# Two transformer blocks on one core: order of the first modulation, of one norm and of the merge's first gate

## The chip, the cores and the metric

The kernel runs on one core of a Trainium2 chip. The metric is the device time of one execution in microseconds, the median of several runs.

## The reference, cut to what matters

Two blocks follow each other on x of 512 tokens by 1024 channels, in float32. Cut to what the change touches:

```python
# first block
mod = silu(c) @ w_ada + b_ada                 # 1024 -> 6144
sh1, sc1, gt1, sh2, sc2, gt2 = split(mod, 6)
h = rmsnorm(x, g_mix) * (1 + sc1) + sh1
proj = h @ w_in                               # q, k, v, pool, gates of a convolution
...
x = x + gt1 * (concat(y_a, y_b, y_c) @ w_out)
h = rmsnorm(x, g_ffn) * (1 + sc2) + sh2
x = x + gt2 * ((silu(h @ w_gate) * (h @ w_up)) @ w_down)
# second block, after a final norm and a feed-forward: ya, yb are its two attentions
...
merged = sigmoid(ga) * (ya @ w_branch_a) + sigmoid(gb) * (yb @ w_branch_b)
h = h + merged @ w_out                        # then the third feed-forward and the last norm
```

`ga` and `gb` are columns of the second block's input projection.

## The kernel before

Activations lie channels by tokens: x is 8 blocks of 128 channels by 512 tokens. Every weight matrix comes in slabs (numbered 0 to 265, mostly 512 KB). Each product is made of three, high by high, high by low and low by high: `split_high(s)` on ScalarE (L1169) rounds a slab to its high half `w_hi`, `split_low(s)` on VectorE (L1567) makes `w_lo` and counts `w_ready`. `w_raw`, `w_hi` and `w_lo` have two buffers each, slab s in s % 2. SP loads slab s when slab s - 2 is split; `split_high(s)` waits until TensorE has used slab s - 2. TensorE's products are lines L564 to L566, whatever the slab. The input has halves too, `h_hi` (ScalarE) and `h_lo` (VectorE), counted by `h_ready`.

Each engine has one program in order, and they meet only at semaphores. PSUM banks are given out ahead of time by `plan`, with what completes and what frees each turn of a bank.

**First modulation.** `sh1` and `sc1` are made on TensorE from `ada_w`, in two halves h of 512 channels: `first_rows(h, ...)` is small products over eight pieces of `ada_w` (L613), `first_columns(h)` turns the row to columns (L624), VectorE (`copy_rows`, `first_mods`) makes the scale, and then for each block k VectorE makes `hm` (L1608), ScalarE `h_hi` (L1188) and VectorE `h_lo` (L1616). The second half's `first_rows(1)` stands inside slab 1 of the value projection (slabs 0 to 3, two blocks k each, four token tiles i each). The other parts of the modulation are summed on VectorE by `mod_step(r)` over rows of `w_ada` that SP brings; `mod_columns` on TensorE (L651) needs eight steps. Slabs 4 and 5 are the first of q and k.

**Norm of the first feed-forward.** The eight chunks `out1` (slabs 28 to 35) are added to x on VectorE (`add_gated`, L1780), squared on ScalarE (`sq`, L1321, two buffers), and summed on the pool engine (`acc`, L2131). TensorE sums over the channels with `mean_d` (L836), ScalarE takes the root (L1357), VectorE the reciprocal, TensorE spreads it over the channels (`spread`, L825), and VectorE and ScalarE make the blocks of h. In between TensorE does `warm(n)`, n products of the identity with itself (L591). Slabs 36 and 37 are the first gate and up slabs.

**Second attention's end and merge.** 32 units t of attention run with half a slab of the input projection each (`part`), scores (L982), transposes (L1000) one unit later, and every fourth unit the values are weighed (`weigh_values`, L957). The last unit's transposes are in round 32, the last weighing in round 33. Then follow per n = 0 to 7 the gate `gb` (slab 182 + 2n) and the two branches (slab 183 + 2n) in `gates`. SP, ScalarE and VectorE go through the slabs in order.

Of the kernel before, what the change touches and what calls it, by code (L numbers as in the profile page):

```python
# [134 lines left out]
def program(nc, ins, out):  # L135
    ctx = ExitStack()
    with ctx:
# [408 lines left out]
        def _(pe):  # L546
# [108 lines left out]
            for s in range(S_V, S_V + 4):  # L655
                await_slab(s)
                for i in range(TT):
                    if s == S_V + 1 and i == 2:
                        first_rows(1, range(KD))
                    if s == S_V + 1 and i == 3:  # L660
                        first_columns(1)
                    b = take(("v1", i)) if s == S_V else i
                    for j in range(2):
                        k = 2 * (s - S_V) + j
                        pe.wait_ge(h_ready, k + 1)
                        ts = slice(P * i, P * i + P)
                        ws = slice(T * j, T * j + T)
                        last = three(psum[:, b, :], h_hi[:, k, ts], h_lo[:, k, ts], w_hi[:, s % 2, ws],
                                     w_lo[:, s % 2, ws], k == 0, k == KD - 1)
                last.then_inc(w_used, 1)  # L670
# [159 lines left out]
            b = take(("sum", "ffn0"))  # L830
            for part_, ready in ((acc[:, 0, :], (summed, SUM0 + KD - 1)), (sq[:, 1, 0, :], (squared, KD))):
                if ready[0] is squared:
                    warm(10)
                pe.wait_ge(*ready)
                for i in range(TT):
                    last = pe.matmul(psum[:, b, i:i + 1], part_[:, P * i:P * i + P], mean_d,  # L836
                                     start=ready[0] is summed and i == 0, stop=ready[0] is squared, skip_group_check=True)
            last.then_inc(filled[b], 1)
            warm(6)
            spread(("scale", "ffn0"), 4, 1)  # L840
            warm(20)

# [99 lines left out]
            def weigh_values(g):  # L942
# [17 lines left out]
                last.then_inc(filled[b], 1)  # L960

            for t in range(UN2 + 2):
                if t < UN2:
# [38 lines left out]


            wait_emptied(pe, ("o2", UN2 // 4 - 1))
            ab = [(ya_hi[:, k, :], ya_lo[:, k, :]) for k in range(4)], [(yb_hi[:, k, :], yb_lo[:, k, :]) for k in range(4)]

            def gates(n, i=None):
                await_slab(S_MERGE + 2 * n, i, 2)
                b = take(("gb",), n, i)
                chunk(psum[:, b, :], S_MERGE, range(KD), hs).then_inc(w_used, 1)  # L1010
                await_slab(S_MERGE + 2 * n + 1, i, 2)
                b = take(("a",), n, i)
                chunk(psum[:, b, :], S_MERGE + 1, range(0, 4), ab[0]).then_inc(filled[b], 1)
                b = take(("b",), n, i)
                chunk(psum[:, b, :], S_MERGE + 1, range(4, 8), ab[1]).then_inc(w_used, 1)
# [141 lines left out]
        def _(act):  # L1157
# [27 lines left out]
            for h in range(PARTS):  # L1185
                for k in range(KP * h, KP * h + KP):
                    act.wait_ge(x_normed, k + 2)
                    act.activation(h_hi[:, k, :], hm[:, k % 2, :], ACT.Identity, bias=modc[:, SH1 + k:SH1 + k + 1])\  # L1188
                       .then_inc(h_high, 1)
                    if k == KP + 1:  # L1190
                        split_high(3)
                if h == 0:
                    split_high(1)
                    split_high(2)
# [318 lines left out]
        def _(dve):  # L1513
# [80 lines left out]
            for h in range(PARTS):  # L1594
# [6 lines left out]
                for k in range(KP * h, KP * h + KP + 1):  # L1601
                    if k == KP + 2:
                        split_low(3)
                    if k < KP * h + KP:
# [14 lines left out]
                if h == 0:  # L1619
                    split_low(1)  # L1620
                    b = wait_filled(dve, "late_vectors")
                    dve.tensor_copy(vcol[:, FIRST_ROWS:N_ROWS], psum[:, b, FIRST_ROWS:N_ROWS]).then_inc(emptied[b], 1)
            dve.wait_ge(lam_landed, 80)
            done(dve.tensor_tensor(lamrow[:, 128:192], lamrow[:, 0:64], lamrow[:, 64:128], ALU.mult))
# [12 lines left out]
            mod_step(1)  # L1637
            for s in range(4, 7):
                split_low(s)
                for r in range(2 * s - 6, 2 * s - 4):  # L1640
                    mod_step(r)
            mod_group(GT1 // KD, KD)

# [148 lines left out]
            for n in range(KD):  # L1792
                wait_emptied(dve, ("side", n))
                add_gated(("out1",), "out1", n, None, GT1)
                if n < KD - 1:
                    split_low(S_OUT1 + n + 2)

            def token_scale(name):
# [263 lines left out]
        def _(pool):  # L2062
# [46 lines left out]
            def sums(phase, clear, kinds=1):  # L2109
# [4 lines left out]
                else:  # L2114

                    pool.memset(acc[:, 0:kinds, :], 0.0).then_inc(summed, 1)
                    pool.wait_ge(summed, SUM0 + SQUARES[phase])
# [10 lines left out]
            pool.wait_ge(summed, SUM0)  # L2128
            for n in range(KD - 1):
                pool.wait_ge(squared, n + 1)  # L2130
# [85 lines left out]
```

## Time and profile before

| | us |
|---|---|
| median of 3 runs | 1731.37 |
| lowest, highest | 1730.52, 1734.26 |
| the profiled execution | 1731.43 |
| its span in the trace | 1729.6 |
| TensorE busy | 1692.3 |
| VectorE busy | 818.6 |
| ScalarE busy | 613.9 |
| pool engine busy | 144.9 |

The rows below come from that one profiled execution, in us from the start of its span. In the timeline a row has the start, the busy time of the instruction or of the merged group, engine, line, operation, output and inputs, the count, and in brackets the idle time ahead of it with what ended it. PE is TensorE, DVE VectorE, ACT ScalarE, POOL the pool engine, SPq the queue that issues transfers. PEclk is the granted clock of TensorE as a part of 2.4 GHz.

### The profile page before, as it was taken

The page shows a single profiled execution, that of the slowest core. Times are in us where ns is not written, and L with a number is a line of the kernel's source. Part 1 is how long each engine was busy: PE and PEld are TensorE (multiplying, and loading weights), DVE is VectorE, ACT ScalarE, POOL GpSimd, SP SyncE. Part 2 cuts the span into 40 slices and gives each one's busy share as a digit, 9 for nine tenths or more (in the row PEclk, how much of TensorE's full clock was granted, in tenths as well). Part 3 has the DMA queues.
Part 4 walks back from the last instruction along what each step waited for, and adds up shares of the span by engine and source line. Part 5 has one row for each costly group of instructions (what it writes and reads, how often), then busy time and mean ns, then how long its engine had stood idle before and what let it go on. Part 6 is the DMA issues. An engine that isn't in the chain of part 4 may idle for free.

```text
span 1729.6 us, 22861 instructions
## 1 busy us (share of the span) xinstructions
PE 1692.3 (98%) x8112; PEld 1368.8 (79%) x8112; DVE 818.6 (47%) x1274; ACT 613.9 (35%) x1063; POOL 144.9 (8%) x151
## 2 busy tenths in 40 slices
PE   7999999999999999999999999999999999999997
PEld 5766688888888887888888887777788888888886
DVE  4788865443333334444443425665455444444232
ACT  3465643222232332222222222555443322223222
POOL 0102111000001131000001130011001100000000
PEclk9999999999999999999999999999999999999999
DMA  9643123443333335333343346122233233333331
GB/s 322 225 134 104 56 80 105 145 121 97 97 111 101 91 90 141 95 97 97 97 125 95 87 141 116 50 62 70 74 97 97 86 97 97 97 97 111 101 100 65
DMA packets 298927, 184.57 MB, mean 107 GB/s; under 512 B 14555, under 2 KB 285335, under 8 KB 298855
## 3 DMA queue, kind: packets, MB, share of 16 engines
q1 hardware_dynamic: 294112, 169.89, 32.9%
q0 software_dynamic: 4400, 13.82, 3.4%
q8 instruction: 34, 0.56, 0.1%
q14 instruction: 21, 0.17, 0.0%
q10 hardware_dynamic: 360, 0.13, 0.0%
HBM read 180.67 MB, written 6.36 MB: 108 GB/s over the span
## 4 chain that ended last, share of the span: by engine, by line
PE 81%; DVE 2%; DMA 1%; ACT 1%; issue 0%; DVEq 0%; ACTq 0%; SPq 0%
PE psum L564 26%; PE psum L566 25%; PE psum L565 25%; PE psum L982 1%; PE psum L957 1%; PE psum L1000 1%; DMA w_raw<-in_ffn_w_gate 1%; DVE w_lo L1567 0%; ACT w_hi L1169 0%; PE psum L816 0%; PE psum L825 0%; PE psum L930 0%; DVE p L1990 0%; PE psum L591 0%; PE psum L836 0%
## 5 line engine op out<-in xcount | busy, mean ns | idle before, releaser
L564 PE MATMUL psum<-h_hi,w_hi 128*128 128x512 f32 x1480 | 585.8, 396 | 7.0 <-DVE w_lo L1567 3.8
L566 PE MATMUL psum<-h_hi,w_lo 128*128 128x512 f32 x1480 | 576.7, 390 | 0.0
L565 PE MATMUL psum<-h_lo,w_hi 128*128 128x512 f32 x1480 | 576.4, 389 | 0.0
L1567 DVE TENSOR_TENSOR w_lo<-w_raw,w_hi 128x1024 fp32r<-128x1024 f32 (+2 forms) x266 | 348.7, 1311 | 308.7 <-ACT w_hi L1169 305.0
L564 PEld LDWEIGHTS psum<-h_hi,w_hi 128*128 128x128 f32 x1480 | 277.7, 188 | 87.2 <-issue 24.6
L1169 ACT ACTIVATE w_hi<-w_raw 128x1024 fp32r<-128x1024 f32 (+2 forms) x266 | 288.1, 1084 | 163.4 <-PE psum L566 148.4
L566 PEld LDWEIGHTS psum<-h_hi,w_lo 128*128 128x128 f32 x1480 | 277.8, 188 | 59.1
L565 PEld LDWEIGHTS psum<-h_lo,w_hi 128*128 128x128 f32 x1480 | 278.0, 188 | 56.3 <-issue 1.0
L564 PE MATMUL psum<-hid_hi,w_hi 128*128 128x512 f32 x528 | 205.5, 389 | 0.0
L566 PE MATMUL psum<-hid_hi,w_lo 128*128 128x512 f32 x528 | 205.4, 389 | 0.0
L565 PE MATMUL psum<-hid_lo,w_hi 128*128 128x512 f32 x528 | 205.4, 389 | 0.0
L1387 ACT ACTIVATE hid_hi<-t_hid 128x512 f32 (+1 forms) x66 | 41.7, 632 | 269.4 <-DVE t_hid L1844 269.4
L2123 POOL TENSOR_TENSOR acc<-acc,sq 128x512 f32<-128x512 f32 x40 | 55.6, 1390 | 719.3 <-ACT sq L1321 718.4
L564 PEld LDWEIGHTS psum<-hid_hi,w_hi 128*128 128x128 f32 x528 | 99.1, 188 | 20.6
L565 PEld LDWEIGHTS psum<-hid_lo,w_hi 128*128 128x128 f32 x528 | 99.1, 188 | 20.6
L566 PEld LDWEIGHTS psum<-hid_hi,w_lo 128*128 128x128 f32 x528 | 99.1, 188 | 20.5
L1844 DVE TENSOR_TENSOR t_hid<-psum,t_silu 128x512 f32<-128x512 f32 x66 | 45.7, 692 | 136.9 <-PE psum L566 134.8
L1382 ACT ACTIVATE t_silu<-t_gate 128x512 f32<-128x512 f32 x44 | 27.8, 632 | 162.2 <-DVE t_gate L1838 162.2
L1848 DVE TENSOR_TENSOR hid_lo<-t_hid,hid_hi 128x512 f32 (+1 forms) x66 | 45.7, 693 | 64.0 <-ACT hid_hi L1387 64.0
L1838 DVE TENSOR_TENSOR t_gate<-psum,rs 128x512 f32<-128x512 f32 x44 | 30.4, 691 | 68.8 <-PE psum L566 68.8
L1229 ACT ACTIVATE p<-p,quad 128x512 f32<-128x512 f32 x64 | 45.6, 715 | 47.8 <-DVE quad L1665 47.8
L1321 ACT ACTIVATE sq<-x_res 128x512 f32 (+1 forms) x40 | 24.9, 622 | 69.4 <-DVE x_res L1907 66.6
(254 smaller groups left out, 1399.8 us busy)
## 6 DMA issues: line engine op xcount, KB each, us to landing
w_raw<-in_w_in SPq DMA_DIRECT2D x50, 512.0 KB, 3.7
w_raw<-in_w_gate_up SPq DMA_DIRECT2D x44, 512.0 KB, 3.7
w_raw<-in_ffn_w_gate SPq DMA_DIRECT2D x44, 512.0 KB, 3.7
w_raw<-in_ffn_w_up SPq DMA_DIRECT2D x44, 512.0 KB, 3.7
w_raw<-in_ffn_w_down SPq DMA_DIRECT2D x32, 704.0 KB, 4.4
w_raw<-in_w_down SPq DMA_DIRECT2D x16, 704.0 KB, 4.4
sq<-in_w_ada SPq DMA_DIRECT2D x20, 512.0 KB, 4.6
ada_w<-in_w_ada SPq DMA_DIRECT2D x16, 512.0 KB, 10.9
```

The source lines that it names most:

```text
L564: pe.matmul(o, a_hi, b_hi, start=start, stop=False)
L565: pe.matmul(o, a_hi, b_lo, start=False, stop=False)
L566: return pe.matmul(o, a_lo, b_hi, start=False, stop=stop)
L1169: act.activation(w_hi[:, s % 2, 0:n], w_raw[:, s % 2, 0:n], ACT.Identity).then_inc(w_high, 1)
L1229: act.activation(p1[:, t % 2, j, m, :], p1[:, t % 2, j, m, :], ACT.Exp, bias=quad[:, t % 2, 4 + at:5 + at], scale=-(2.0 ** -(2 * c + j + 1 ...
L1382: act.activation(t_silu[:, :], t_gate[:, :], ACT.Silu).then_inc(gate_act, 1)
L1387: act.activation(hid_hi[:, slot_of(n, i), :], t_hid[:, :], ACT.Identity).then_inc(hid_high, 1)
L1567: dve.tensor_tensor(w_lo[:, s % 2, 0:n], w_raw[:, s % 2, 0:n], w_hi[:, s % 2, 0:n].bitcast(F32), ALU.subtract).then_inc(w_ready, 1)
L1838: dve.tensor_tensor(t_gate[:, :], psum[:, b, :], rs[:, :], ALU.mult).then_inc(gate_scaled, 1)
L1844: dve.tensor_tensor(t_hid[:, :], psum[:, b, :], t_silu[:, :], ALU.mult).then_inc(hid_set, 1)
L1848: dve.tensor_tensor(hid_lo[:, at, :], t_hid[:, :], hid_hi[:, at, :].bitcast(F32), ALU.subtract)\
L2123: pool.tensor_tensor(acc[:, m, :], acc[:, m, :], sq[:, n, m, :], ALU.add).then_inc(summed, 1)
```

## The change

It has three parts. In the first modulation, `first_rows(1)` and `first_columns(1)` stand one token tile earlier in slab 1; `split_high(3)` stands one block later on ScalarE; `split_low(3)` stands behind the last block on VectorE, and `mod_step` 6 and 7 stand ahead of `split_low(6)`. In the norm, the pool engine sums six blocks instead of seven, TensorE sums blocks 6 and 7 straight from `sq`, the ten warming products between the sums are gone, and the other two groups are 3 and 14 instead of 6 and 20; `split_low` of slab 36 stands behind the last addition to x. In the merge, the first gate (`gb`, 0) is made in two halves of twelve products, one in round 32 behind the last transposes and one in round 33 behind the last weighing.

```diff
--- before.py
+++ after.py
@@ -655,9 +655,9 @@
             for s in range(S_V, S_V + 4):
                 await_slab(s)
                 for i in range(TT):
+                    if s == S_V + 1 and i == 1:
+                        first_rows(1, range(KD))
                     if s == S_V + 1 and i == 2:
-                        first_rows(1, range(KD))
-                    if s == S_V + 1 and i == 3:
                         first_columns(1)
                     b = take(("v1", i)) if s == S_V else i
                     for j in range(2):
@@ -828,17 +828,16 @@
 
             pe.wait_ge(*free_at[("sub", 3)])
             b = take(("sum", "ffn0"))
-            for part_, ready in ((acc[:, 0, :], (summed, SUM0 + KD - 1)), (sq[:, 1, 0, :], (squared, KD))):
-                if ready[0] is squared:
-                    warm(10)
+            for part_, ready in ((acc[:, 0, :], (summed, SUM0 + KD - 2)), (sq[:, 0, 0, :], (squared, KD - 1)),
+                                 (sq[:, 1, 0, :], (squared, KD))):
                 pe.wait_ge(*ready)
                 for i in range(TT):
                     last = pe.matmul(psum[:, b, i:i + 1], part_[:, P * i:P * i + P], mean_d,
-                                     start=ready[0] is summed and i == 0, stop=ready[0] is squared, skip_group_check=True)
+                                     start=ready[0] is summed and i == 0, stop=ready == (squared, KD), skip_group_check=True)
             last.then_inc(filled[b], 1)
-            warm(6)
+            warm(3)
             spread(("scale", "ffn0"), 4, 1)
-            warm(20)
+            warm(14)
 
             def ffn(f, sums, spreads):
                 s0 = S_GU[f]
@@ -958,6 +957,16 @@
                                              wt2[:, j, slot:slot + nq, :].rearrange("p s q -> p (s q)"),
                                              start=n == 0, stop=n == len(group) - 1)
                 last.then_inc(filled[b], 1)
+
+            def first_gate(q):
+
+                if q == 0:
+                    await_slab(S_MERGE)
+                    take(("gb", 0))
+                last = chunk(psum[:, bank_of(("gb", 0)), :], S_MERGE, range(4 * q, 4 * q + 4), hs[4 * q:4 * q + 4], None,
+                             q == 0, q == 1)
+                if q == 1:
+                    last.then_inc(w_used, 1)
 
             for t in range(UN2 + 2):
                 if t < UN2:
@@ -1001,13 +1010,17 @@
                         last.then_inc(filled[b], 1)
 
 
+                if t >= UN2:
+                    first_gate(t - UN2)
+
             wait_emptied(pe, ("o2", UN2 // 4 - 1))
             ab = [(ya_hi[:, k, :], ya_lo[:, k, :]) for k in range(4)], [(yb_hi[:, k, :], yb_lo[:, k, :]) for k in range(4)]
 
             def gates(n, i=None):
-                await_slab(S_MERGE + 2 * n, i, 2)
-                b = take(("gb",), n, i)
-                chunk(psum[:, b, :], S_MERGE, range(KD), hs).then_inc(w_used, 1)
+                if n:
+                    await_slab(S_MERGE + 2 * n, i, 2)
+                    b = take(("gb",), n, i)
+                    chunk(psum[:, b, :], S_MERGE, range(KD), hs).then_inc(w_used, 1)
                 await_slab(S_MERGE + 2 * n + 1, i, 2)
                 b = take(("a",), n, i)
                 chunk(psum[:, b, :], S_MERGE + 1, range(0, 4), ab[0]).then_inc(filled[b], 1)
@@ -1187,7 +1200,7 @@
                     act.wait_ge(x_normed, k + 2)
                     act.activation(h_hi[:, k, :], hm[:, k % 2, :], ACT.Identity, bias=modc[:, SH1 + k:SH1 + k + 1])\
                        .then_inc(h_high, 1)
-                    if k == KP + 1:
+                    if k == KP + 2:
                         split_high(3)
                 if h == 0:
                     split_high(1)
@@ -1599,8 +1612,6 @@
                 dve.wait_ge(mod_set, h + 1)
                 b = wait_filled(dve, "x_scale")
                 for k in range(KP * h, KP * h + KP + 1):
-                    if k == KP + 2:
-                        split_low(3)
                     if k < KP * h + KP:
                         wait_emptied(dve, ("x", k))
                         if k >= 2:
@@ -1620,6 +1631,7 @@
                     split_low(1)
                     b = wait_filled(dve, "late_vectors")
                     dve.tensor_copy(vcol[:, FIRST_ROWS:N_ROWS], psum[:, b, FIRST_ROWS:N_ROWS]).then_inc(emptied[b], 1)
+            split_low(3)
             dve.wait_ge(lam_landed, 80)
             done(dve.tensor_tensor(lamrow[:, 128:192], lamrow[:, 0:64], lamrow[:, 64:128], ALU.mult))
             dve.tensor_reduce(lamrow[:, 192:194], lamrow[:, 128:192].rearrange("p (a d) -> p a d", a=2),
@@ -1635,10 +1647,13 @@
             g0, f0 = ROW_OF["g_final"], ROW_OF["ffn1_norm_2"]
             dve.tensor_tensor(gff[:, :], vcol[:, g0:g0 + KD], vcol[:, f0:f0 + KD], ALU.mult).then_inc(lam_set, 1)
             mod_step(1)
-            for s in range(4, 7):
+            for s in (4, 5):
                 split_low(s)
                 for r in range(2 * s - 6, 2 * s - 4):
                     mod_step(r)
+            for r in (6, 7):
+                mod_step(r)
+            split_low(6)
             mod_group(GT1 // KD, KD)
 
 
@@ -1792,8 +1807,9 @@
             for n in range(KD):
                 wait_emptied(dve, ("side", n))
                 add_gated(("out1",), "out1", n, None, GT1)
-                if n < KD - 1:
+                if n < KD - 2:
                     split_low(S_OUT1 + n + 2)
+            split_low(S_GU[0])
 
             def token_scale(name):
 
@@ -2113,7 +2129,7 @@
                     done(pool.memset(acc[:, 0:kinds, :], 0.0))
                 else:
 
-                    pool.memset(acc[:, 0:kinds, :], 0.0).then_inc(summed, 1)
+                    pool.memset(acc[:, 0:kinds, :], 0.0).then_inc(summed, 2)
                     pool.wait_ge(summed, SUM0 + SQUARES[phase])
                 with repeat(pool, KD // 2, []) as i:
                     for n in range(2):
@@ -2126,7 +2142,7 @@
             wait_filled(pool, ("mod", SC2 // KD))
             pool.memset(acc[:, 0, :], 0.0).then_inc(summed, SUM0)
             pool.wait_ge(summed, SUM0)
-            for n in range(KD - 1):
+            for n in range(KD - 2):
                 pool.wait_ge(squared, n + 1)
                 pool.tensor_tensor(acc[:, 0, :], acc[:, 0, :], sq[:, n % 2, 0, :], ALU.add).then_inc(summed, 1)
                 pool.wait_ge(summed, SUM0 + n + 1)
```

## Rows read from the trace of the kernel before

**Rows 1.** The page's part 1, busy time of the engines.

```profile
PE 1692.3 (98%) x8112; PEld 1368.8 (79%) x8112; DVE 818.6 (47%) x1274; ACT 613.9 (35%) x1063; POOL 144.9 (8%) x151
```

**Rows 2.** Waits of TensorE: us in total, times, longest.

```profile
PE psum L564 <- DVE h_lo L1616: 6.3, 4, 2.3
```

**Rows 3.** Timeline, second half of the first modulation: start, us, engine, line.

```profile
36.40 3.66 PE L613 MATMUL psum<-ada_w,cact_wide 128*32 128x256 f32 x64
...
44.21 0.75 DVE L1616 SCALAR_TENSOR_TENSOR h_lo<-hm,modc,h_hi 128x512 fp32r<-128x512 f32 x1 [0.20 <-ACT h_hi L1188]
...
45.11 0.47 PE L564 MATMUL psum<-w_hi,h_hi 128*128 128x512 f32 x1 [1.62 <-DVE h_lo L1616]
...
45.75 1.23 DVE L1567 TENSOR_TENSOR w_lo<-w_raw,w_hi 128x1024 fp32r<-128x1024 f32 x1 [0.79 <-ACT w_hi L1169]
...
47.00 0.50 SPq L1060 DMA_DIRECT2D w_raw<-in_w_in  x1
...
48.35 0.80 PE L564 MATMUL psum<-w_hi,h_hi 128*128 128x512 f32 x1 [2.31 <-DVE h_lo L1616]
```

**Rows 4.** Stretches of that time: busy (count) of each engine, PEclk, DMA, GB/s.

```profile
48.00:51.00 3.00, 2.65 (x6) 2.15 (x7) 2.67 (x6) 1.11 (x2) 0.00 (x0) 0.55 1.02 373
51.00:55.00 4.00, 4.00 (x17) 3.24 (x16) 2.59 (x7) 1.49 (x2) 3.65 (x7) 0.91 1.07 379
```

**Rows 5.** Timeline, first half of the modulation.

```profile
18.36 1.16 PE L634 MATMUL psum<-ident,rcol 128*128 128x128 f32 x8 [1.23 <-DVE rcol L1534]
...
25.65 0.47 PE L564 MATMUL psum<-w_hi,h_hi 128*128 128x512 f32 x1 [1.88 <-DVE h_lo L1616]
...
27.08 0.50 PE L564 MATMUL psum<-w_hi,h_hi 128*128 128x512 f32 x1 [0.49 <-DVE h_lo L1616]
```

**Rows 6.** Tile `ada_w`, its last two transfers.

```profile
L1047 SPq DMA_DIRECT2D ada_w<-in_w_ada x2: 1166/1200/1235, 21.1 to 22.4; - x2
...
DMA to landing us min/median/max: 11.0/11.1/11.1
```

**Rows 7.** Timeline around the end of slab 5.

```profile
60.45 2.07 ACT L1201 ACTIVATE v<-psum 128x512 f32<-128x512 f32 x4 [4.32 <-PE psum L566]
...
71.47 1.92 PE L651 MATMUL psum<-small,acc 128*128 128x1 f32 x16 [0.18 <-issue]
```

**Rows 8.** Transfers issued in 46.9 to 47.6: count, KB, us to landing.

```profile
w_raw<-in_w_in SPq DMA_DIRECT2D x1, 512.0 KB, 7.7
```

**Rows 9.** Timeline, norm of the first feed-forward.

```profile
264.41 0.63 ACT L1321 ACTIVATE sq<-x_res 128x512 f32<-128x512 f32 x1 [1.97 <-POOL acc L2131]
...
264.52 1.02 PE L836 MATMUL psum<-small,acc 128*128 128x1 f32 x8 [1.06 <-POOL acc L2131]
...
266.53 1.52 PE L836 MATMUL psum<-small,sq 128*128 128x1 f32 x8
...
269.22 1.92 PE L825 MATMUL psum<-ident,rcol 128*128 128x128 f32 x8
...
272.91 0.75 DVE L1824 SCALAR_TENSOR_TENSOR h_lo<-x_scaled,modc,h_hi 128x512 fp32r<-128x512 f32 x1 [0.26 <-ACT h_hi L1364]
...
274.32 0.47 PE L564 MATMUL psum<-h_hi,w_hi 128*128 128x512 f32 x1
```

**Rows 10.** Timeline, end of the second attention and merge.

```profile
1218.12 0.70 PE L1000 MATMUL psum<-ident,p 128*128 128x128 f32 x4 [0.81 <-DVE p L1974]
...
1219.47 1.96 PE L957 MATMUL psum<-wt,vp 128*64 128x128 f32 x28 [0.66 <-ACT wt L1467]
...
1222.85 0.50 PE L564 MATMUL psum<-h_hi,w_hi 128*128 128x512 f32 x1 [1.41 <-DVE ya_lo L2010]
...
1223.05 1.23 DVE L1567 TENSOR_TENSOR w_lo<-w_raw,w_hi 128x1024 fp32r<-128x1024 f32 x1 [0.25 <-ACT w_hi L1169]
...
1228.42 0.39 PE L564 MATMUL psum<-ya_hi,w_hi 128*128 128x512 f32 x1
```

**Rows 11.** A stretch of the norm, columns as in rows 4.

```profile
273.00:275.00 2.00, 2.00 (x15) 1.78 (x13) 2.00 (x4) 1.07 (x2) 0.00 (x0) 0.86 1.01 319
```

## The prediction

> **What bounds the kernel now.** I read the shares of the page first: TensorE is busy for 1692.3 of 1729.6 us [rows 1], so only some 37 us can be had without removing products. Next came the waits of TensorE: the largest sum is for blocks of the modulated input's low half, 6.3 us in four waits [rows 2]. Then I read the timeline around each of the three places that the diff touches, and the stretches with the granted clock, because a stall also costs when the clock falls behind it. All matmuls of the weight slabs run at 0.23 us each: the 24 products of the first gate chunk start at 1222.85 and the next chunk at 1228.42, which is 5.57 us [rows 10]. Between the three places TensorE waits little, so what it gains in one of them is still there at the end.
>
> **First modulation, before.** The 64 small products of the second half's modulation (`first_rows(1)`) start at 36.40 and take 3.66 us; from them follow, in a chain on VectorE and ScalarE, `h_lo` of block 4, done at 44.21 + 0.75 = 44.96. TensorE starts slab 2 at 45.11, 1.62 us idle. Then VectorE makes the low half of slab 3 (45.75, 1.23 us, itself behind an idle of 0.79 for ScalarE's high half) before it goes on with block 5, and TensorE gets its next product at 48.35, 2.31 us idle [rows 3]. After these two stalls the granted clock is at its lower level, 1.2 GHz: 0.55 on average in 48 to 51 and 0.91 in 51 to 55 [rows 4]. That is 2 x 0.45 x 3 + 2 x 0.09 x 4 = 3.4 us at the lower level.
>
> **The change there.** (a) The 64 products start one token tile earlier, that is six products, 6 x 0.23 = 1.4 us, and everything of the chain with them. TensorE reaches the end of slab 1 at the same time as now (about 43.5), because the products are only in another order; block 4 is ready at 43.6 and the wait falls from 1.6 to about 0.25. Gain 1.4. Cover: the last two pieces of `ada_w` are issued at 21.1 and 22.4 and take 11.0 to 11.1 us to land, so by 33.5 [rows 6]; the products would start at 35.0. If the data came x us after 35.0 the gain would be 1.4 - x. (b) Slab 3's low half leaves the place ahead of block 5. Nothing then stands between blocks 4 and 5. The same pair of blocks in the first half, where nothing stands there, has TensorE's products at 25.65 and 27.08, 1.43 us apart [rows 5]; here it is 48.35 - 45.11 = 3.24. Gain 1.8. Slab 3's low half now follows block 7: blocks 5, 6 and 7 take some 1.4, 1.5 and 1.2 us after 43.6, so it runs at about 47.5 to 48.8. TensorE wants slab 3 after the 21 products that are left of slab 2, from 45.1: at 49.9. Cover 1.1 us. ScalarE's high half, one block later, is done by 46.1. (c) With idles of 0.25 and about 0.5 the clock should stay at 2.4 GHz; 3.4 us at half speed cost 1.7 us. Gain 1.7, or zero if it falls as before. (d) The accumulation steps 6 and 7 of the modulation row go ahead of slab 6's low half. Today `mod_columns` begins at 71.47, 0.18 us idle [rows 7]. With the steps 1.2 us earlier this wait goes: 0.2. Slab 6's own low half ends as late as the steps do now, about when slab 5's products end; ahead of its first use stand the column products (1.92 us) and the scores, so it is covered. Sum: 1.4 + 1.8 + 1.7 + 0.2 = 5.1; I take 5.0, and 3.3 without the clock.
>
> The queues there: SP loads slab 5 once slab 3's low half is made. It was issued at 47.00 [rows 3] and took 7.7 us to land, behind four rows of `w_ada` [rows 8]. Now it goes at 48.8, the rows about 1.4 us earlier than before. With 7.7 again it lands at 56.5. ScalarE splits it behind the four copies of `v1` (2.07 us from 60.45 now, [rows 7]), which move to about 55.4: at 57.5. Cover 1.0 us, and the shorter queue gives more. Slabs 4, 6 and 7 are released by low halves that move with TensorE or ahead of it. Rows 6 and 7 are issued after step 0 and are wanted near 62, some 12 us later.
>
> **Norm of the first feed-forward, before.** The last `out1` product ends at about 263.46. The sums over `acc` start at 264.52, 1.06 us idle for the pool engine's seventh addition; ten warming products follow, and only at 266.53 the four products over the last square, which take 1.52 us. That square was ready at 264.41 + 0.63 = 265.04. Six warming products more, the spread at 269.22 (1.92 us), and the first `h_lo` at 272.91 + 0.75 = 273.66. TensorE begins at 274.32, since 20 warming products still run [rows 9].
>
> **The change there.** The pool engine adds six blocks, done at about 261; block 6's square (262.4) and block 7's (265.04) are summed by TensorE. Removed: the wait of 1.06 and ten warming products. Added: four products with `sq[0]`, 1.02 us by the row of `acc`'s, 0.9 from start to start. With 2.4 GHz `acc` takes 263.3 to 264.2, `sq[0]` to 265.1, `sq[1]` 265.15 to 266.2. The root, the reciprocal and the signals between took 269.22 - 268.05 = 1.17, of which 0.5 was the tail of six warming products; with three it is about 0.7. Spread from 266.9: at 2.4 GHz I take 1.16 us, the time of the first spread (L634) at 18.36 [rows 5]. End 268.0 against 271.14: 3.1. At 1.2 GHz sums and spread together cost up to 1.1 more: 2.0. What counts is the end of the spread and not the 0.6 us by which the warming products overran: block 2's `h_lo` is what VectorE delivers last before TensorE is fed, and it moves with the spread. I take 2.6 between the ends, since the sums (one column each) and three warming products leave little array work there. Slab 36's low half behind the last addition to x takes 1.2 us, ready at 265.6, with the reciprocal at 266.7: covered. It gains nothing ahead of that addition either, which today waits for TensorE. SP's load released by it goes 2.2 us later and is wanted 18 us later. The pool engine issues its `w_ada` rows 2 us earlier, on no path.
>
> The granted clock is 0.86 in 273 to 275, so it rose while TensorE ran only identity products; the first real one starts at 274.32 [rows 9, 11]. The Trainium skill, "TensorE: Matmul & The Clock Gate", Part 4, says that the full clock does not engage for transposes. The trace disagrees; by that rule the warming products would be worth nothing, cutting them would be free, and the first gate and up products would begin at 1.2 GHz. By it the norm would give the 2.0 of the lower end and the time would be 1722.5; how long the clock would then stay low is the rival that ends slower.
>
> **Merge, before.** The last transposes start at 1218.12, then 0.66 us idle, the last weighing (1219.47, 1.96 us), then 1.41 us idle for the last `ya_lo`, then the gate at 1222.85 [rows 10]. **After:** twelve gate products go ahead of the weighing, twelve behind it. Its slab is split by 1216.1 and its bank was read before, so they need nothing. They take 2.8 us each time: the weighing runs 1221.6 to 1223.5 and the second half to 1226.3. Both idles go, 2.07. In their place comes slab 183: ScalarE's and VectorE's halves of it stand behind `ya_hi` and `ya_lo`, and its low half ended at 1223.05 + 1.23 = 1224.28, 2.85 us after the weighing's end [rows 10]; now that is 1226.4, and the branch products wait 0.1. Gain 1.95. The 0.81 us ahead of the last transposes stay. SP's load of slab 185 is released 2.1 us later, 1226.4, is there by 1231, and is wanted at 1231.9: cover 0.9.
>
> **The sum.** 5.0 + 2.6 + 1.95 = 9.55 us. The profiled execution took 1731.43 us, 0.06 over the median of 1731.37: 1731.43 - 9.5 = 1721.9 us, 0.55% faster. What a measurement of this kernel can tell from no change is 0.2%, 3.5 us.
>
> **The rivals.**
> - All three gains come, 0.76. Its own range: without the clock's part in the first stage and with the norm at 1.2 GHz 1731.43 - 7.25 = 1724.2; with all at the best ends 1721.2.
> - A new wait in the first stage, 0.08: slab 5 lands late. For: the cover is 1.0 us, and TensorE wants it 5 us earlier. Against: the rows ahead of it in the queue go earlier. At a landing at 60 ScalarE's and VectorE's halves end at 62.3, against a demand at 60.6: 1.7 lost, 1723.6; if it or `ada_w` costs the whole first part, 1726.9.
> - The merge's wait only moves, 0.06: the branch products wait for slab 183 by as much as was saved. 1723.9. Against: its chain is known to 0.1 us.
> - Two of the places give nothing, 0.06: 1728 or so.
> - Slower, 0.04: the clock. With 19 warming products fewer (36 to 17), it stays at 1.2 GHz into the first gate and up chunks. A product then takes 0.44 us [rows 4] in place of 0.23, 0.2 more. The gains are used up after 9.5 / 0.2 = 48 products, which are the first two chunks exactly; four chunks would give 1731.4 - 9.5 + 19 = 1741. Against: the low stretch behind the two stalls ended by itself after 3.4 us [rows 4], that of the norm before its first real product [rows 9, 11].
>
> **Chances and range.** Faster by over 0.2%: 0.90; within 0.2%: 0.06; slower: 0.04. The range 1718.5 to 1727.0 holds the first rival and the second and third, with the error of my 0.1 and 0.2 us steps; it leaves out the last two and half of the tails.
>
> **What would show it.** Slab 2's first product some 1.4 us earlier and its second within 1.5 us of it; no low clock between 45 and 55; slab 3's low half ahead of TensorE's need; `mod_columns` without idle; the spread 2 to 3 us earlier against the last `out1` product; no idle after the weighing and at most 0.3 us ahead of the branch products. The prediction is wrong if the clock falls in a new place, or if TensorE waits for `w_lo` of slabs 3, 5 or 183.

## The result, and the profile after

The changed kernel took 1721.87 us in the median of 4 runs (1720.81 to 1722.97), the kernel before 1732.24 in 4 (1730.52 to 1734.26). The ratio is 0.9941, with a 95% interval of 0.9927 to 0.9955: 0.6% faster, clear of the 0.2% that the prediction took as the least that a measurement can tell. The forecast was 1721.9. On another chip the two were timed again, with 1722.2 against 1732.96 (ratio 0.9938, 0.9924 to 0.9951).

The profiled execution of the changed kernel took 1721.02 us, its span is 1719.2. Its page, part 1:

```profile
PE 1688.0 (98%) x8101; PEld 1364.4 (79%) x8101; DVE 817.5 (48%) x1274; ACT 613.6 (36%) x1063; POOL 143.0 (8%) x150
```

TensorE's busy time fell by 4.3 us and its idle time in the span from 37.3 to 31.2 [rows 1]. The first part is product time at the lower clock and the warming products that are gone. Its waits, with us in total, times and longest; the first row answers to [rows 2], where it was 6.3 us:

```profile
PE psum L564 <- DVE h_lo L1627: 3.1, 4, 1.9
...
PE psum L1009 <- DVE p L1990: 0.8, 1, 0.8
PE psum L613 <- DMA ada_w<-in_w_ada: 0.7, 1, 0.7
...
PE psum L956 <- ACT wt L1480: 0.2, 1, 0.2
```

The wait for the last `ya_lo`, 1.41 us before [rows 10], is in no row any more. The second half of the first modulation, from the timeline (compare [rows 3]; lines have moved, L1580 is `w_lo`, L1627 `h_lo`, L1073 SP's load):

```profile
34.92 3.66 PE L613 MATMUL psum<-ada_w,cact_wide 128*32 128x256 f32 x64
...
42.74 0.75 DVE L1627 SCALAR_TENSOR_TENSOR h_lo<-hm,modc,h_hi 128x512 fp32r<-128x512 f32 x1 [0.20 <-ACT h_hi L1201]
...
43.64 0.47 PE L564 MATMUL psum<-w_hi,h_hi 128*128 128x512 f32 x1 [0.25 <-DVE h_lo L1627]
...
45.07 0.50 PE L564 MATMUL psum<-w_hi,h_hi 128*128 128x512 f32 x1 [0.50 <-DVE h_lo L1627]
...
47.44 1.22 DVE L1580 TENSOR_TENSOR w_lo<-w_raw,w_hi 128x1024 fp32r<-128x1024 f32 x1
...
48.69 0.38 SPq L1073 DMA_DIRECT2D w_raw<-in_w_in  x1
```

The two idles of 1.62 and 2.31 us are 0.25 and 0.50, and slab 3's low half stands behind the last block. The end of slab 5 in the timeline (compare [rows 7]): `mod_columns` has no idle in front.

```profile
66.32 1.84 PE L651 MATMUL psum<-small,acc 128*128 128x1 f32 x16
```

The clock in 40 to 48 and 48 to 55, columns as in [rows 4], is full:

```profile
40.00:48.00 8.00, 7.25 (x33) 5.39 (x32) 6.90 (x13) 3.67 (x5) 0.18 (x1) 1.00 0.65 203
48.00:55.00 7.00, 7.00 (x33) 5.79 (x32) 5.99 (x12) 2.44 (x3) 6.59 (x13) 1.00 1.00 345
```

The norm, from the timeline (compare [rows 9]), and two stretches of it:

```profile
258.05 0.94 PE L835 MATMUL psum<-small,acc 128*128 128x1 f32 x8
...
258.86 2.07 PE L835 MATMUL psum<-small,sq 128*128 128x1 f32 x16
...
261.50 1.28 PE L825 MATMUL psum<-ident,rcol 128*128 128x128 f32 x8 [0.18 <-DVE rcol L1817]
...
262.57 3.19 PE L591 MATMUL psum<-ident 128*128 128x128 f32 x14
...
264.55 0.75 DVE L1840 SCALAR_TENSOR_TENSOR h_lo<-x_scaled,modc,h_hi 128x512 fp32r<-128x512 f32 x1 [0.26 <-ACT h_hi L1377]
...
265.45 0.65 PE L564 MATMUL psum<-h_hi,w_hi 128*128 128x512 f32 x1
```

```profile
262.00:264.00 2.00, 2.00 (x13) 2.00 (x13) 1.67 (x3) 0.28 (x1) 0.61 (x2) 0.60 0.99 292
264.00:266.00 2.00, 2.00 (x11) 1.90 (x10) 1.74 (x4) 1.06 (x3) 0.00 (x0) 0.55 0.91 283
```

All sums run straight behind the last `out1` product. In the two stretches, the granted clock is the third number from the end. In this execution the clock fell only while the spread was under way (at 262.4; the spread took 1.28 us, against 1.92 before), and it was back at full at 265.8, just behind the start of the first gate product (265.45). The end of the attention and the merge (compare [rows 10]):

```profile
1209.48 0.70 PE L1009 MATMUL psum<-ident,p 128*128 128x128 f32 x4 [0.81 <-DVE p L1990]
...
1209.94 0.49 PE L564 MATMUL psum<-h_hi,w_hi 128*128 128x512 f32 x1
...
1212.89 1.96 PE L956 MATMUL psum<-wt,vp 128*64 128x128 f32 x28
...
1214.79 0.50 PE L564 MATMUL psum<-h_hi,w_hi 128*128 128x512 f32 x1
...
1216.48 1.23 DVE L1580 TENSOR_TENSOR w_lo<-w_raw,w_hi 128x1024 fp32r<-128x1024 f32 x1 [0.25 <-ACT w_hi L1182]
...
1217.81 0.47 PE L564 MATMUL psum<-ya_hi,w_hi 128*128 128x512 f32 x1
```

Twelve gate products stand in front of the weighing and twelve behind it, and the branch products follow 0.10 us behind the end of slab 183's low half.

**Where the time went.** I cut the span at marks that every kernel has. Stage A runs from the first value product (slab 0) to the start of `mod_columns`, stage N from the last `out1` product to the first `t_silu` on ScalarE, stage M from the last transposes to the first branch product. The stretches between are called A to N, N to M, and tail.

| us | before | changed | difference |
|---|---|---|---|
| A (25.65 to 71.47; 25.71 to 66.32) | 45.82 | 40.61 | 5.21 |
| A to N | 191.59 | 191.50 | 0.09 |
| N (263.07 to 286.62; 257.82 to 278.29) | 23.55 | 20.47 | 3.08 |
| N to M | 931.50 | 931.19 | 0.31 |
| M (1218.12 to 1228.42; 1209.48 to 1217.81) | 10.30 | 8.33 | 1.97 |
| tail | 501.21 | 501.40 | -0.19 |

With the 0.06 us by which the first value product came later this is 10.41, all of 1731.43 - 1721.02.

### The profile page after: what moved, and what is told of

Its sections match the earlier page's. It is cut to its first block, busy times and chain, and to the rows that moved or that the text cites. A ratio compares the mean times of both kernels' runs of the same rounds, so it can differ in the third digit from the quotient of the medians.

```text
span 1719.2 us, 22837 instructions
## 1 busy us (share of the span) xinstructions
PE 1688.0 (98%) x8101; PEld 1364.4 (79%) x8101; DVE 817.5 (48%) x1274; ACT 613.6 (36%) x1063; POOL 143.0 (8%) x150
## 4 chain that ended last, share of the span: by engine, by line
PE 91%; DVE 5%; ACT 2%; issue 1%; DMA 1%; DVEq 0%; ACTq 0%; SPq 0%
PE psum L564 28%; PE psum L566 28%; PE psum L565 28%; PE psum L991 1%; PE psum L956 1%; PE psum L1009 1%; DMA w_raw<-in_ffn_w_gate 1%; DVE p L1733 1%; DVE w_lo L1580 1%; PE psum L770 1%; PE psum L730 1%; ACT p L1242 1%; PE psum L746 0%; DVE acc L1573 0%; DVE p L1672 0%
## 5 line engine op out<-in xcount | busy, mean ns | idle before, releaser
L1580 DVE TENSOR_TENSOR w_lo<-w_raw,w_hi 128x1024 fp32r<-128x1024 f32 (+2 forms) x266 | 348.5, 1310 | 305.6 <-ACT w_hi L1182 301.9
```

The lines of the kernel that those rows point to most:

```text
L1580: dve.tensor_tensor(w_lo[:, s % 2, 0:n], w_raw[:, s % 2, 0:n], w_hi[:, s % 2, 0:n].bitcast(F32), ALU.subtract).then_inc(w_ready, 1)
```

## The experiments

The same stages, from one profiled execution of each kernel. (For r1_three the mark of M, the last transposes, has six gate products moved in front of it, so its N to M and M do not compare with the rest.)

| kernel | A | A to N | N | N to M | M | tail |
|---|---|---|---|---|---|---|
| before | 45.82 | 191.59 | 23.55 | 931.50 | 10.30 | 501.21 |
| p1_modulation | 40.73 | 193.20 | 23.67 | 931.81 | 10.35 | 501.31 |
| q1_rows | 44.37 | 191.64 | 23.64 | 931.32 | 10.35 | 501.26 |
| q2_slab3 | 42.43 | 191.61 | 23.50 | 931.46 | 10.31 | 501.28 |
| p2_norm | 45.72 | 191.61 | 21.23 | 931.34 | 10.32 | 502.79 |
| q3_sums | 45.53 | 192.98 | 21.22 | 931.25 | 10.30 | 502.62 |
| p3_gate | 45.41 | 192.94 | 23.50 | 931.19 | 8.33 | 502.94 |
| p3_again | 46.25 | 194.55 | 21.72 | 931.49 | 8.33 | 503.32 |
| p23_norm_gate | 45.41 | 192.95 | 21.22 | 931.20 | 8.33 | 501.41 |
| changed | 40.61 | 191.50 | 20.47 | 931.19 | 8.33 | 501.40 |
| a1_after | 40.23 | 191.51 | 20.89 | 931.47 | 8.33 | 503.08 |
| q4_nowarm | 41.01 | 192.52 | 21.20 | 931.92 | 8.33 | 503.07 |
| r1_three | 40.76 | 194.78 | 20.33 | 931.85 | 6.84 | 501.37 |

### The three parts alone

**p1_modulation**: before, with the first modulation's edits:

```diff
+                    if s == S_V + 1 and i == 1:
+                        first_rows(1, range(KD))
                     if s == S_V + 1 and i == 2:
-                        first_rows(1, range(KD))
-                    if s == S_V + 1 and i == 3:
                         first_columns(1)
...
-                    if k == KP + 1:
+                    if k == KP + 2:
                         split_high(3)
...
-                    if k == KP + 2:
-                        split_low(3)
...
+            split_low(3)
             dve.wait_ge(lam_landed, 80)
...
-            for s in range(4, 7):
+            for s in (4, 5):
                 split_low(s)
                 for r in range(2 * s - 6, 2 * s - 4):
                     mod_step(r)
+            for r in (6, 7):
+                mod_step(r)
+            split_low(6)
```

> The first modulation's part alone (rows one token tile earlier, slab 3's halves behind, steps 6 and 7 ahead of slab 6), the rest as before. Theory, that the stalls removed add up: 5.1 us less, with mod_columns some 5.2 us earlier and no low clock between 40 and 55, and the norm and the merge with their old idles. Rival, that the later stages give part of it back through slab 5 or the queues: under 3.5 us less in all, though mod_columns starts 5 us earlier. Rival, that most of the gain is the clock: the idles of 1.62 and 2.31 stay near 1.6 and 0.5 and the time falls by under 3.

Measured: 1727.56 against 1732.45, ratio 0.9966 (0.9952 to 0.998). The medians are 4.9 us apart, the ratio gives 5.9, between 3.5 and 8.3. Stage A is 40.73, within 0.15 us of the whole change's; N and M are as before. The later stages take nothing of the gain but for 1.6 us in A to N, and that is a low stretch of the clock: in 160 to 175 it is 0.89 on average (3.3 us at 1.2 GHz), where the kernel before has 1.00. The theory holds. The rival of slab 5 and the queues fails, and so does that of the clock: the two idles are 0.25 and 0.50.

**p2_norm**: before, with the norm's edits (sums, pool engine's six blocks, warming products, slab 36's low half):

```diff
-            for part_, ready in ((acc[:, 0, :], (summed, SUM0 + KD - 1)), (sq[:, 1, 0, :], (squared, KD))):
-                if ready[0] is squared:
-                    warm(10)
+            for part_, ready in ((acc[:, 0, :], (summed, SUM0 + KD - 2)), (sq[:, 0, 0, :], (squared, KD - 1)),
+                                 (sq[:, 1, 0, :], (squared, KD))):
...
-            warm(6)
+            warm(3)
             spread(("scale", "ffn0"), 4, 1)
-            warm(20)
+            warm(14)
...
```

> The norm's part alone: six blocks on the pool engine, two on TensorE, 17 warming products in place of 36, slab 36's low half behind the last addition to x. Theory: 3.1 us less where the clock falls behind the spread or not at all, 2.0 where sums and spread run at 1.2 GHz. Rival, that the gain is all in the clock: nothing, or more than 4 us, by whether it falls. Rival, that the removed warming products were needed: a low clock into the first gate and up products, 0.2 us lost on each.

Measured: 1731.36 against 1732.45, ratio 0.9991 (0.9981 to 1.0). Stage N is 21.23 against 23.55, 2.3 us shorter. In this execution the spread ran at 1.2 GHz in full (2.07 us), so this is the forecast's lower end and 0.3 more. The clock was low from 266.6 to 270.0 there, for 3.4 us against 6.8 in the kernel before (266.7 to 273.5), and full when the gate products began, so the rival of the missing warming products fails. How much of the gain is clock is told below. The times say less than the stage: the medians are 1.1 us apart, and the interval runs from no change to 3.3 us.

**p3_gate**, and the same kernel again as **p3_again**: before, with `first_gate` and the `if n:` in `gates`, as in the diff of the change.

> The merge's part alone: the first gate in two halves around the last weighing. Theory: 1.95 us less, no idle ahead of the weighing, 0.1 ahead of the branch products. Rival, that the wait only moves to slab 183: under 0.5 us less, with an idle of 1.5 or more ahead of the branch products.

> The merge's part alone a second time, because its first timing showed 1.1 us in the medians where the stretch from the last transposes to the branch products is 2.0 shorter. Theory, that the rest is chance in where the low clock falls (72 to 76 and the last 20 us): 2 us less than before in the mean of the runs, about 1730.2, and that stretch again 2.0 shorter. Rival, that the earlier merge brings more low clock elsewhere: again 1 us or less, with a lower mean clock than before's runs.

Measured: ratios 0.9995 (0.9986 to 1.0005) and 0.9993 (0.9984 to 1.0002); medians 1.1 and 1.7 us less than before. Stage M is 8.33 in both executions, 1.97 to 2.02 shorter than in the kernels with the old order, and it is 8.33 in all six executions with the two halves. The stage says 2.0. The times alone can't: both intervals hold 2 us less (the lower ends are 2.4 and 2.8) as well as no change. The means of p3_again's runs and of those beside it are 1731.3 and 1732.7, 1.4 us apart, between the theory's 2 and the rival's 1; their mean clock is 0.993 in both, so what the rival named as its sign is not there.

**p23_norm_gate**: both parts together.

> The norm's and the merge's parts together, the first modulation as before. Theory, that the stages add up: 2.3 for the norm (as in the norm's part alone) and 2.0, so 4.3 us less than before, about 1728. Rival, that these two parts give their gain only beside the first modulation's: 2.2 us less, the sum of the two medians measured alone.

Measured: 1728.94 against 1732.99, ratio 0.9976 (0.9967 to 0.9985), 4.2 us, between 2.6 and 5.7. The stages give 2.3 and 2.0, so 4.3. The rival's 2.2 lies outside. The parts add up without the first one: N and M are the same as in the single parts.

### The first modulation, edit by edit

**q1_rows** has the first piece of the diff of p1_modulation alone, **q2_slab3** only the moves of slab 3's two halves.

> Only the rows and columns products one token tile earlier; slab 3's halves and the steps where they were. Theory: the wait for block 4 falls by 1.4 to 0.25, that for block 5 stays at about 1.8 to 2.3, since slab 3's low half still stands ahead of it. 1.4 us less if the clock still falls behind the second wait, 3.1 if it doesn't. Rival, that the two edits do the same work twice: nearly 5 us less with this one alone.

> Only slab 3's high half one block later and its low half behind block 7. Theory: the wait for block 4 stays at 1.6, that for block 5 falls from 2.3 to 0.5; 1.8 us less if the clock still falls, 3.5 if it does not. Rival, that slab 3's low half now comes too late: a wait for w_lo of over 0.5 us ahead of slab 3's first product, and 1.3 us less at most.

Measured: q1_rows 1729.47 against 1732.5, ratio 0.998 (0.997 to 0.999); stage A 44.37. q2_slab3 1727.91, ratio 0.9973 (0.9961 to 0.9986); stage A 42.43. The idles, from the timelines of q1_rows (first) and q2_slab3 (second):

```profile
43.27 0.47 PE L564 MATMUL psum<-w_hi,h_hi 128*128 128x512 f32 x1 [0.25 <-DVE h_lo L1616]
...
44.21 1.23 DVE L1567 TENSOR_TENSOR w_lo<-w_raw,w_hi 128x1024 fp32r<-128x1024 f32 x1 [1.09 <-ACT w_hi L1169]
...
46.81 0.80 PE L564 MATMUL psum<-w_hi,h_hi 128*128 128x512 f32 x1 [2.61 <-DVE h_lo L1616]
```

```profile
45.05 0.47 PE L564 MATMUL psum<-w_hi,h_hi 128*128 128x512 f32 x1 [1.62 <-DVE h_lo L1614]
...
46.48 0.51 PE L564 MATMUL psum<-w_hi,h_hi 128*128 128x512 f32 x1 [0.49 <-DVE h_lo L1614]
```

The stretch behind them, with the granted clock third from the end, first of q1_rows and then of q2_slab3:

```profile
48.00:52.00 4.00, 4.00 (x15) 3.16 (x14) 3.10 (x10) 1.85 (x3) 2.19 (x4) 0.74 1.05 374
```

```profile
48.00:52.00 4.00, 4.00 (x19) 3.34 (x18) 2.98 (x6) 1.53 (x4) 2.47 (x5) 1.00 1.02 376
```

Each edit removes its own wait and leaves the other as it was: with the rows moved, the wait for block 5 is even 2.61, because VectorE now waits 1.09 us for ScalarE's half of slab 3. The clock follows the second edit: one idle of 2.61 us still brought it down, one of 1.62 followed by 0.49 did not. All thirteen profiled executions agree with that. In the seven with slab 3's low half in front of block 5 the clock is at 1.2 GHz somewhere between 45 and 53 us, for 3.4 us (before, p2_norm, q1_rows) or 6.8 (the others); in the six with it behind block 7 it is full from 40 to 60. A shortens by 1.45 and 3.39, in sum 4.84; the rest of the 5.2 is the 0.18 us in front of `mod_columns` and the scatter of 0.1 to 0.2 that A shows where the clock falls at the same places (A differs by up to 0.8 where it doesn't). Neither rival holds: the edits don't do the same work twice, and slab 3 is never late. The times of q1_rows show more than its stage, though: 3.0 us between the medians, 1.7 to 5.2 by the interval, against 1.45. The mean clock of its runs was 0.995, that of the kernel before beside them 0.994, so part of it is likely clock elsewhere; no trace here shows where.

### The norm: sums or warming products?

**q3_sums** is before with the new sums, but the old 6 and 20 warming products:

```diff
-            warm(3)
+            warm(6)
             spread(("scale", "ffn0"), 4, 1)
-            warm(14)
+            warm(20)
```

(The diff is against p2_norm.)

> The norm's sums as changed (no products between them), but 6 and 20 warming products behind as before; the rest as before. Theory: the extra three products ahead of the spread cost 0.3 to 0.6 us at most, the six extra behind it 0 to 0.6 since block 2's low half sets the pace: 2 to 3 us less than before. Rival, that the cut of the warming products is what gives the gain: under 1 us less. Rival, that more warming products keep the clock up: 3.5 us less and no low clock in the norm.

Measured: ratio 0.9998 (0.9988 to 1.0009), which resolves nothing, but stage N is 21.22, as p2_norm's 21.23, and 2.3 shorter than before. Both spreads ran at 1.2 GHz (2.07 us), so the two compare. Cutting 3 and 6 warming products gives nothing; the new sums, with the ten products between them gone and slab 36's low half moved, give it all. But the whole time doesn't follow: the interval runs from 1.6 us slower to 2.1 us faster and leaves the stage's 2.3 just outside. The mean clock of its runs was 0.993 against 0.994 beside them, so low clock elsewhere may have taken part of the gain; that was not traced.

**q4_nowarm** is the changed kernel without any of them:

```diff
-            warm(3)
             spread(("scale", "ffn0"), 4, 1)
-            warm(14)
```

> The whole change, with the 3 and the 14 warming products of the norm taken away as well. Theory, that the warming products count for the clock: a low stretch behind the spread that reaches into the first gate and up products, 1 to 3 us slower than the changed kernel, about 1724. Rival, the skill's rule that the full clock does not engage for transposes: no difference from the changed kernel, or 0.2 us faster, since the spread need not wait for three of them.

Measured: 1724.27 in the median of 4, against 1721.87 and 1722.2 for the changed kernel. Two of its waits, the second one in the norm, and its stretches there:

```profile
PE psum L613 <- DMA ada_w<-in_w_ada: 2.7, 4, 1.0
PE psum L564 <- DVE h_lo L1838: 2.7, 1, 2.7
```

```profile
264.00:266.00 2.00, 0.00 (x0) 0.00 (x0) 1.74 (x3) 1.16 (x2) 0.00 (x0) 0.55 0.98 279
266.00:268.00 2.00, 1.44 (x4) 1.04 (x5) 2.00 (x4) 0.89 (x2) 0.00 (x0) 0.50 0.97 293
268.00:271.00 3.00, 3.00 (x9) 2.14 (x9) 3.00 (x6) 1.45 (x2) 0.00 (x0) 0.50 0.68 217
```

TensorE idles for 2.7 us where the warming products were, and the clock is at 1.2 GHz from 264.2 to 271.0, over the first gate products (9 in 3 us, where the changed kernel has 17 in 4). In the changed kernel the low stretch lasted 3.4 us, from 262.4 to 265.8, and TensorE ran the end of the spread and the 14 identity products in it. N is 21.20. That is 0.9 us longer than in r1_three below, whose spread also ran at full clock (1.16 us in both). It is no longer than in p2_norm, q3_sums and p23_norm_gate, which have warming products but lost 0.9 us in a spread at 1.2 GHz. The helper `warm` issues its products as transposes (`pe.transpose`). So this speaks against the rule of the Trainium skill ("TensorE: Matmul & The Clock Gate", Part 4: PE-mode transpose) that the full clock does not engage for transpose mode: where the idle held them, the low stretch was half as long. The kernels were timed on different chips, and their ratios to the kernel before (0.9945, 0.9928 to 0.9961, against 0.9938 and 0.9941) overlap, so the 2 us between the medians are an indication only.

### One step further

**a1_after** is the changed kernel again; **r1_three** makes the first gate in three pieces:

```diff
+                if t == UN2:
+                    first_gate(0, 2)
                 u = t - 1
                 if 0 <= u < UN2:
                     for j in range(2):
                         pe.wait_ge(combined2, 2 * u + j + 1)
...
-                if t >= UN2:
-                    first_gate(t - UN2)
+                if t == UN2:
+                    first_gate(2, 4)
+                elif t > UN2:
+                    first_gate(4, KD)
```

> The changed kernel again, as the measure for the next one on the same chip: 10 us less than before, its runs in two groups some 1.9 us apart by whether the norm's sums and spread run at 1.2 GHz.

> The changed kernel with the first gate in three pieces: six products ahead of the last transposes, six behind them, twelve behind the last weighing. Theory, that any product fills any idle ahead of it: the 0.81 us ahead of the last transposes go too, 0.7 to 0.8 us less than the changed kernel, unless the weighing then waits for ScalarE's copies: six products take 1.4 us and that wait was 0.66, so it should not. Rival, that the chain of slab 183 decides: the idle comes back ahead of the branch products, no gain.

Measured, on the same chip: 1722.2 (1720.75 to 1722.63) and 1720.62 (1719.82 to 1723.39), against 1732.96 before; ratios 0.9938 (0.9924 to 0.9951) and 0.993 (0.9917 to 0.9944). The runs of a1_after do lie in two groups (1720.75 and 1721.03; 1722.2 to 1722.63), but not for the reason expected: its profiled execution, of the slower group, is 1.61 us longer than that of the changed kernel above, with 0.42 more in the norm, 0.38 less in A and 1.68 more in the tail. The timeline of r1_three:

```profile
1211.54 0.60 PE L1010 MATMUL psum<-ident,p 128*128 128x128 f32 x4
...
1211.90 0.48 PE L564 MATMUL psum<-h_hi,w_hi 128*128 128x512 f32 x1
...
1212.68 0.40 PE L564 MATMUL psum<-h_hi,w_hi 128*128 128x512 f32 x1
...
1213.37 0.60 PE L1010 MATMUL psum<-ident,p 128*128 128x128 f32 x4
...
1213.73 0.48 PE L564 MATMUL psum<-h_hi,w_hi 128*128 128x512 f32 x1
...
1214.51 0.39 PE L564 MATMUL psum<-h_hi,w_hi 128*128 128x512 f32 x1
...
1215.30 1.96 PE L956 MATMUL psum<-wt,vp 128*64 128x128 f32 x28
```

The idle of 0.81 in front of the last transposes is gone and the weighing has none. From the transposes before them to the first branch product it is 1220.21 - 1211.54 = 8.67 us, in the changed kernel 1217.81 - 1208.08 = 9.73, so 1.06 shorter: the 0.81 and small starts. The slab-183 rival fails. In the times the two overlap; the gain over the changed kernel is shown by the stage and not by the medians, though its median is the lowest of the kernels that ran.

## Why the prediction was right

**First modulation, 5.0 forecast, 5.2 measured.** (a) The rows started at 34.92 (35.0 forecast), and the wait of 1.62 became 0.25, as said; q1_rows shows it alone. The cover named for this step was too good, though. The last piece of `ada_w` was issued at 22.9 and took 13.7 us, so it landed at about 36.6 and not by 33.5; TensorE wanted it at about 37.8 (estimated from the even starts of the 64 products between 34.9 and 38.2). q4_nowarm shows the loss that the prediction called x: there TensorE had no low stretch between 22 and 40 (the changed kernel has one of 3.4 us from 26.9, and the kernel before a like one), reached the rows at 33.31, sat idle for 0.97 us until the last piece came at 37.5, and block 4's wait was 0.93 in place of 0.25. (b) The second product of the pair came 1.43 us behind the first, the distance of the first half; q2_slab3 shows it alone. Slab 3's low half ran from 47.44 to 48.66 (47.5 to 48.8 forecast), SP's load of slab 5 went at 48.69 (48.8), and nothing waited for it. (c) The clock stayed at full, and the thirteen executions show that it hung on edit (b). (d) `mod_columns` lost its 0.18.

**Norm, 2.6 forecast between 2.0 and 3.1, 3.1 measured.** The steps came as listed: no idle in front of the sums, the spread 3.45 us behind their start and at 1.16 to 2.07 us by the clock. The size hung on the clock, which is why the forecast stood between two ends; the measured executions lie at 2.3 (p2_norm, q3_sums, p23_norm_gate), 2.7 (a1_after) and 3.1 (changed). What the prediction had not separated is that the kernel before also paid for the clock. p3_again has the old norm, and in its execution the clock did not fall there; from the timeline:

```profile
267.20 1.02 PE L836 MATMUL psum<-small,acc 128*128 128x1 f32 x8 [1.06 <-POOL acc L2145]
...
269.21 0.95 PE L836 MATMUL psum<-small,sq 128*128 128x1 f32 x8
...
270.80 1.16 PE L825 MATMUL psum<-ident,rcol 128*128 128x128 f32 x8
```

The stretch around it, at full clock:

```profile
262.00:274.00 12.00, 10.94 (x79) 9.66 (x77) 5.98 (x9) 4.74 (x8) 4.21 (x4) 1.00 0.53 157
```

There N is 21.72; r1_three, with the new norm and no low clock in it either, has 20.33. So the order of the sums is worth 1.4 us, and the clock costs the old norm 1.8 to 1.95 where it fell and the new one up to 0.9. Each of these is a difference of single executions. Of the 3.1 us between the two profiled kernels about 1.4 is order and 1.7 clock.

**Merge, 1.95 forecast, 1.97 measured.** Both idles went, and the branch products follow the low half of slab 183 as worked out. Beside slab 183's end at 1217.71 the first branch product at 1217.81 shows how little was left to gain behind the weighing.

**Sum.** 1721.9 forecast, 1721.87 measured. The nearness is partly luck. The gain itself was 10.4 us, by the medians as by the two profiled executions, against 9.5 forecast: the norm gave 0.5 more than taken, the first stage 0.2, and the rest of the kernel 0.15. It did not show in the time, since the median of the kernel before came out at 1732.24, 0.8 above the profiled execution that the forecast started from. And the same kernel's runs lie up to 2 us apart (1720.75 to 1722.97).

**The rivals.** Slab 5 was not late: its low half began at 58.69, the copies of `v1` had begun at 55.64 as reckoned. The merge's wait did not move. Slower by a low clock in the first gate products did not come with the 14 warming products, but q4_nowarm shows the mechanism: 6.8 us of low clock cost 0.9 us in the stage.

## What to carry to other kernels

Where one engine is busy for 98%, look for idles of 0.3 to 3 us in it and put work that needs nothing of the late data in front of each; with the norm's and the merge's parts together, each stage came out within 0.02 us of what it was alone. Price a stall together with the clock behind it: here 3.2 us less idle in front of two products gave 5.0. When the effect is 2 us in 1730, cut the trace at fixed marks and compare stages: single runs of one kernel lie up to 6 us apart, where the merge's stage repeats to 0.05. A stage shows what an edit does there; it doesn't show what the clock does elsewhere, and the medians of q1_rows and q3_sums differ from their stages by 1.5 us, one up and one down. Compare a stage only between executions in which the clock fell at the same places.

## What the runs showed of the hardware

- The lower clock does not always fall at the same places, not even for one kernel. p3_gate and p3_again are the same kernel: in p3_gate the clock was at 1.2 GHz from 267.4 to 274.2, in p3_again it stayed full in the norm (stage N 23.50 and 21.72), and A to N was 192.94 and 194.55. The stretch A to N is 191.5 to 191.6 us in six executions and 192.5 to 194.8 in seven; the tail is 501.2 to 501.4 in seven and 502.6 to 503.3 in six. The scatter of 1728.5 to 1734.4 us in the kernel before goes with the clock: of its 71 runs beside the experiments, the fifteen with a mean granted clock of 0.992 took 1732.6 to 1734.4, the ten with 0.996 or 0.997 1728.5 to 1730.8. The Trainium skill ("TensorE: Matmul & The Clock Gate", Part 1) says that the point at which the full clock comes is variable from run to run. Here that is so also of whether and where it falls.
- In the norm the clock fell in eleven of thirteen executions. In the old order (before, p1_modulation, q1_rows, q2_slab3, p3_gate) it fell in the second group of sums and stayed low for 6.8 us. In the new order (p2_norm, q3_sums, p23_norm_gate, changed, a1_after) it fell 0.5 to 1.5 us behind the end of the sums, in the spread or 0.1 us ahead of it, and stayed low for 3.4. In the changed kernel TensorE is shown busy without a break in 262 to 264 and 264 to 266 (2.00 of 2.00 us in both), with a clock of 0.60 and 0.55.
- With the identity products in the norm the clock was back at full within 0.4 us of the first gate product in the changed kernel (265.8 against 265.45), and before it in the kernel before, in p2_norm and in a1_after. Without them, in q4_nowarm, it was at 1.2 GHz for 6.8 us, the last 4.4 of them over gate products.
